# Feed-forward down product of a decoder trunk: two passes of eight output tiles, or seven block products

## The chip, the cores and the metric

The kernel runs on one core of a Trainium2 chip. The metric is device time in microseconds of one execution. Before the change the median of three runs is 2619.1 us (2617.98 to 2620.26).

## The reference, cut to what matters

One decoder layer over 2048 tokens of width 1024: RMSNorm, a token mixer of three head groups (gated linear attention, a recurrent branch, dilated attention), residual; then RMSNorm, a gated feed-forward with a short convolution, residual, and a last RMSNorm. The change touches the last part, and one idle engine inside the dilated attention.

```python
u = rms_norm(x2, norm_ffn) @ w_up            # (2048, 1024) @ (1024, 5632)
u = causal_dwconv(u, conv_w, conv_b)         # width 3
a = gelu(gate) * value                       # (2048, 2816), gate and value are the halves of u
x3 = x2 + a @ w_down                         # (2048, 2816) @ (2816, 1024)
out = rms_norm(x3, norm_final)
```

## The kernel before, in words

All tensors are transposed: channels on the 128 partitions, tokens along the free dimension, in blocks of 512 (NB). A product in float32 is made of three TensorE passes: ScalarE writes a rounded copy ("hi") of each operand, VectorE subtracts it from the raw one ("lo"), and `three_passes` (L2069 to L2071) multiplies hi by hi, hi by lo and lo by hi. Each pass is one matmul of 128x128 weights by 128x512 data.

The program runs four functions in turn: `mixer_front`, `dilated_attention`, `output_projection` and `conv_ffn`. The last takes over half of the time. It works through the tokens in two halves of 1024 (two blocks of 512 each).

**Up stage of a half** (22 pairs g of a value tile and a gate tile): the up product is already done as seven block products per pair (names A00, S1, S2, A01, S3, A11, S4 in `ORDER`), 84 matmuls per pair. GpSimd makes the sums of weights (`sums_of_slab`, `last_sum_of_slab`), ScalarE and VectorE split nine products ahead into a ring of 11 slots (`high_w` L2481, `low_w` L2629). ScalarE keeps partial sums (`keep`, L2491), VectorE moves the four blocks out of PSUM (`move`, L2646 to L2652), ScalarE applies the middle tap (`tap`, L2500), VectorE the two other taps (`convolve`, L2667), ScalarE the GELU (L2505), and VectorE multiplies value by gate (`multiply`, L2674). SyncE stores the product to DRAM (`store_a`, L2247).

**Down stage of a half**: 44 steps (two passes over the 22 tiles of the inner dimension). A pass makes four of the eight output tiles for both token blocks, in all eight PSUM banks. A step loads one weight tile (256 KB) and one activation tile (512 KB) (`load_step`, L2256 and L2258), splits both (`high_step` L2514, L2515; `low_step` L2679, L2681), and runs 24 matmuls (`down`). Raw operands and split operands have two buffers each. After a pass VectorE adds the residual (`drain`, L2689), ScalarE squares (L2524), GpSimd sums the squares (`totals`, L2403); the first four output tiles are written to a scratch tensor x3_t and read again later, since the RMS is known only after the second pass. `sum_squares` (L2811) sums over partitions with a matrix of ones, `root` (L2533, L2535) makes the reciprocal root, `invert` (L2696) and GpSimd (L2427, L2449) scale the output.

Every engine runs its list in the order in which it is written, and waits for semaphores on the way. So the order in the code is the order of the work. The loop over pairs in the vector engine's program ends with the last pair's work in the order: move, `low_step(half, 0)`, move, gate taps, move, `low_step(half, 1)`, value taps, multiply, then the steps from 2 on. SyncE's list has `store_a` of the last pair ahead of the loads of step 2.

**Dilated attention**: 40 turns j; in the first 16 (`TILES_0`) the keys and queries are read in place; GpSimd stages keys only from turn 16 on (`stage`, L1387), and has nothing else to do until then. VectorE works on PSUM (maxima L1531, copies L1537, sums taken L1554, L1556), SyncE stores values and sums of each turn (`store_values` L1310, `store_sums` L1306).

## Time and profile before

| what | value |
|---|---|
| median of 3 runs | 2619.1 us |
| the profiled execution's own time | 2608.52 us |
| its span, first to last instruction | 2606.7 us |
| mean granted TensorE clock | 0.971 |
| dilated attention | from about 683 to 985 us of the span |
| output projection | about 1003 to 1190 us |
| down stage, first half | starts at 1645 us |
| down stage, second half | 2330 to 2581 us |

The profiled execution ran 10.6 us below the median of the runs shown. Matmuls are pipelined: the "busy" time of TensorE says little about its pace, the count of matmuls in a stretch says more. Where a wait is said to end with some engine, that was inferred from the semaphores.

### The profile page before, as it was taken

To read this page: it belongs to the slowest core of one execution; us is meant where nothing else is said; L and a number is where in the kernel's file an instruction comes from. 1 tells how busy PE (TensorE), PEld (TensorE's weight loads), DVE (VectorE), ACT (ScalarE), POOL (GpSimd) and SP (SyncE) were. 2 spreads that over 40 slices of the span, in tenths; PEclk is the share of its full clock that TensorE was granted. 3 is DMA by queue.
4 is the path that set the end of the run, shared out by engine and by line. 5 is a ranking of instruction groups with operands and counts; after the bars stand their busy time and mean duration, and the time that the engine had idled before them with its cause. 6 is when DMAs were issued, how large, how long until landed. Compare 5 with 4: busy or idle time off the path is not lost.

```text
span 2606.7 us, 32959 instructions
## 1 busy us (share of the span) xinstructions
PE 2468.8 (95%) x12224; PEld 1991.9 (76%) x12224; DVE 1557.8 (60%) x2159; ACT 1083.9 (42%) x1859; POOL 736.3 (28%) x648
## 2 busy tenths in 40 slices
PE   7999999999799996995999999899989999999996
PEld 5777777777578775874888888788868888877885
DVE  6554456774355774354777777445567877763434
ACT  6434353332247553124444444225454444432432
POOL 4111104340004761223333332012044534310103
PEclk9999999999899998997999999999999999999998
DMA  4232325442514226354222122465513222224463
GB/s 161 97 109 91 102 88 163 150 148 71 194 57 142 90 78 237 122 186 181 87 82 89 73 96 83 140 210 199 170 73 134 101 89 81 74 87 158 163 242 125
DMA packets 149279, 327.27 MB, mean 126 GB/s; under 512 B 12656, under 2 KB 56704, under 8 KB 141440
## 3 DMA queue, kind: packets, MB, share of 16 engines
q1 hardware_dynamic: 149120, 325.17, 36.3%
q8 instruction: 98, 1.61, 0.3%
q14 instruction: 61, 0.50, 0.1%
HBM read 231.55 MB, written 93.57 MB: 125 GB/s over the span
## 4 chain that ended last, share of the span: by engine, by line
PE 47%; DVE 3%; POOL 1%; ACT 1%; DMA 1%; issue 1%; SPq 0%; POOLq 0%; ACTq 0%; DVEq 0%
PE ff_bank L2069 16%; PE ff_bank L2071 16%; PE ff_bank L2070 16%; DVE ff_y L2667 1%; POOL ffn_rstd L2403 1%; DVE ff_b_lo L2624 1%; POOL ff_x_last L2449 0%; DMA ff_a_raw<-a_t 0%; DMA ff_b_raw<-h_t 0%; ACT ff_y L2500 0%; DVE ff_ring L2629 0%; DVE ff_x2d L2689 0%; DVE ff_a_lo L2681 0%; ACT ff_a_hi L2515 0%; DMA out_t<-ff_x2d 0%
## 5 line engine op out<-in xcount | busy, mean ns | idle before, releaser
L2069 PE MATMUL ff_bank<-ff_b_hi,ff_ring 128*128 128x512 f32 x1232 | 483.9, 393 | 33.5 <-DVE ff_b_lo L2624 13.5
L2071 PE MATMUL ff_bank<-ff_b_hi,ff_ring 128*128 128x512 f32 x1232 | 482.3, 391 | 0.0
L2070 PE MATMUL ff_bank<-ff_b_lo,ff_ring 128*128 128x512 f32 x1232 | 482.2, 391 | 0.0
L66 PE MATMUL ip_bank<-ip_x_hi,ip_w_hi 128*128 128x512 f32 x736 | 302.2, 411 | 19.5 <-DVE ip_x_lo L701 16.1
L2069 PEld LDWEIGHTS ff_bank<-ff_b_hi,ff_ring 128*128 128x128 f32 x1232 | 233.1, 189 | 87.0 <-issue 32.7
L2069 PE MATMUL ff_bank<-ff_a_hi,ff_w_hi 128*128 128x512 f32 x704 | 276.8, 393 | 16.7 <-DVE ff_a_lo L2681 16.5
L67 PE MATMUL ip_bank<-ip_x_lo,ip_w_hi 128*128 128x512 f32 x736 | 292.5, 397 | 0.0
L68 PE MATMUL ip_bank<-ip_x_hi,ip_w_lo 128*128 128x512 f32 x736 | 291.4, 396 | 0.0
L2667 DVE SCALAR_TENSOR_TENSOR ff_y<-ff_u,ff_conv_all,ff_y 128x1024 f32<-128x1024 f32 x176 | 240.3, 1365 | 63.0 <-ACT ff_y L2500 59.8
L2070 PE MATMUL ff_bank<-ff_a_lo,ff_w_hi 128*128 128x512 f32 x704 | 276.0, 392 | 0.0
L2071 PE MATMUL ff_bank<-ff_a_hi,ff_w_lo 128*128 128x512 f32 x704 | 275.8, 392 | 0.0
L2070 PEld LDWEIGHTS ff_bank<-ff_b_lo,ff_ring 128*128 128x128 f32 x1232 | 233.2, 189 | 48.7 <-issue 0.2
L2071 PEld LDWEIGHTS ff_bank<-ff_b_hi,ff_ring 128*128 128x128 f32 x1232 | 233.0, 189 | 48.9
L2629 DVE TENSOR_TENSOR ff_ring<-ff_raw,ff_ring 128x512 fp32r<-128x512 f32 x220 | 177.1, 806 | 61.0 <-ACT ff_ring L2481 61.0
L2679 DVE TENSOR_TENSOR ff_w_lo<-ff_w_raw,ff_w_hi 128x512 fp32r<-128x512 f32 x88 | 63.9, 727 | 245.6 <-ACT ff_w_hi L2514 245.6
L66 PEld LDWEIGHTS ip_bank<-ip_x_hi,ip_w_hi 128*128 128x128 f32 x736 | 141.4, 192 | 56.2 <-issue 15.0
L2514 ACT ACTIVATE ff_w_hi<-ff_w_raw 128x512 fp32r<-128x512 f32 x88 | 55.6, 632 | 304.8 <-PE ff_bank L2071 276.0
L2069 PEld LDWEIGHTS ff_bank<-ff_a_hi,ff_w_hi 128*128 128x128 f32 x704 | 133.5, 190 | 46.8 <-DVE ff_a_lo L2681 18.7
L2500 ACT ACTIVATE ff_y<-ff_u,ff_conv_all 128x1024 f32<-128x1024 f32 x88 | 109.6, 1245 | 135.8 <-DVE ff_u L2650 101.3
L67 PEld LDWEIGHTS ip_bank<-ip_x_lo,ip_w_hi 128*128 128x128 f32 x736 | 141.7, 193 | 30.6 <-issue 2.6
L68 PEld LDWEIGHTS ip_bank<-ip_x_hi,ip_w_lo 128*128 128x128 f32 x736 | 141.5, 192 | 30.7
L1450 ACT ACTIVATE at_probs<-at_s,at_neg 128x256 f32<-128x256 f32 (+1 forms) x288 | 108.1, 437 | 135.6 <-DVE at_neg L1531 121.7
(248 smaller groups left out, 4388.6 us busy)
## 6 DMA issues: line engine op xcount, KB each, us to landing
ff_a_raw<-a_t SPq DMA_DIRECT2D x88, 512.0 KB, 4.2
ff_raw<-in_slabs SPq DMA_DIRECT2D x43, 1024.0 KB, 4.8
proj_t<-ip_staged SPq DMA_DIRECT2D x92, 256.0 KB, 2.7
a_t<-ff_y SPq DMA_DIRECT2D x44, 512.0 KB, 2.6
ff_w_raw<-in_w_down SPq DMA_DIRECT2D x88, 256.0 KB, 2.7
rp_tables<-in_rope SPq DMA_DIRECT2D x24, 512.0 KB, 4.4
ip_w_raw<-in_w_in SPq DMA_DIRECT2D x23, 512.0 KB, 4.0
at_qkv<-proj_t SPq DMA_DIRECT2D x12, 768.0 KB, 12.0
```

Of the source, the lines that this page charges most:

```text
L66: pe.matmul(out, w_hi[k], x_hi[k], start=(k == 0), stop=False)
L67: pe.matmul(out, w_hi[k], x_lo[k], start=False, stop=False)
L68: last = pe.matmul(out, w_lo[k], x_hi[k], start=False, stop=(k == n - 1))
L1450: ins = act.activation(probs[:, g, at], scores_at(j, g)[:, hh, n * c:n * (c + 1)], ACT.Exp, bias=neg[:, j % 2, c, 2 * g + hh:2 * g + hh + 1])
L2069: pe.matmul(out, w_hi, x_hi, start=first, stop=False, skip_group_check=resumed)
L2070: pe.matmul(out, w_hi, x_lo, start=False, stop=False, skip_group_check=resumed)
L2071: return pe.matmul(out, w_lo, x_hi, start=False, stop=last, skip_group_check=resumed)
L2500: act.activation(y[:, a, :], u[:, a, TAPS - 1:], ACT.Identity, bias=conv_all[:, g, a, TAPS:TAPS + 1], scale=conv_all[:, g, a, TAPS - 1:TAP ...
L2514: act.activation(w_hi[n % 2][:, :], w_raw[n % 2][:, :], ACT.Copy).then_inc(d_hi_ready, 1)
L2629: dve.tensor_tensor(ring[:, M % RING, 1, :], source(half, m), ring[:, M % RING, 0, :].bitcast(F32), ALU.subtract).then_inc(w_lo_ready, 1)
L2667: dve.scalar_tensor_tensor(out=y[:, a, :], in0=u[:, a, t:t + HALF], scalar=conv_all[:, g, a, t:t + 1], in1=y[:, a, :], op0=ALU.mult, op1=A ...
L2679: dve.tensor_tensor(w_lo[n % 2][:, :], w_raw[n % 2][:, :], w_hi[n % 2][:, :].bitcast(F32), ALU.subtract).then_inc(d_lo_ready, 1)
```

## The change

- **Down product**: the output of a half is taken as a 2x2 matrix of blocks (four output tiles by 512 tokens), the inner dimension as 11 (`KP`) pairs of tiles. Instead of eight block products it makes seven (`DOWN`), each over 11 steps: 77 steps of 12 matmuls. A step loads one weight tile and one activation tile of 512 tokens, 256 KB each. Raw operands get three buffers, split ones four, in slots of the ring.
- **Sums of weights** (`s_t`, four per pair of tiles): made by GpSimd during the first 16 turns of the attention, in a ring of three, loaded and stored by SyncE between its other transfers.
- **Sums of gated activations** (`t_t`): VectorE makes four per two pairs (`sums_of_gated`), one after an even pair, three after an odd one; ScalarE keeps one block before it is overwritten. SyncE stores them.
- **Partial results**: ScalarE copies the first product out (`keep_first_product`), GpSimd adds it to three quarters of the residual (`add_first_product`), VectorE drains six groups of four tiles.
- **Output**: all eight output tiles of a half stay in SBUF, so the scratch x3_t, its store and its loads go away, and so does GpSimd's scaling (L2427, L2449). The second token block is squared, summed and scaled inside the last steps. For the last block of all, the last four squares are summed over partitions by TensorE directly, one matmul of the ones matrix each.
- **End of the up stage**: step 0's split stands earlier, step 1's too, a third step is split ahead; `store_a` of the last pair and its sums are stored after the loads of step 8.

The core of the diff:

```diff
+W_RING = 3
+            def load_weights(i):
+                if i >= W_RING:
+                    sp.wait_ge(w_stored[i % W_RING], 16 * (i // W_RING))
+                for m in range(2):
+                    sp.dma_start(w_sums[:, i % W_RING, 2 * m:2 * m + 2, :], w_down[m, 2 * i:2 * i + 2].rearrange("k p c -> p k c")
+                                 ).then_inc(w_in[i % W_RING], 16)
+            def store_weights(i):
+                sp.wait_ge(w_summed, 4 * (i + 1))
+                sp.dma_start(s_t[i], w_sums[:, i % W_RING, :, :]).then_inc(w_stored[i % W_RING], 16)
             for j in range(TURNS):
+                if 0 <= j - 5 < KP:
+                    store_weights(j - 5)
+                if 0 <= j - 3 < KP:
+                    load_weights(j - 3)
                 if j < TILES_0:
                     store_values(j)
...
+            def sum_weights(i):
+                pool.wait_ge(neg_saved, i + 3)
+                pool.wait_ge(w_in[i % W_RING], 32 * (i // W_RING + 1))
+                at = w_sums[:, i % W_RING, :, :]
+                pool.tensor_tensor(at[:, 3, :], at[:, 2, :], at[:, 3, :], ALU.add).then_inc(w_summed, 1)
...
+            for i in range(KP):
+                sum_weights(i)
             for j in range(TILES_0 - 1, TURNS + 4):
...
+        DOWN = [("A11", "B11", 0, True), ("A12", "B21", 0, False), ("S2", "T2", 1, True), ("S1", "T1", 0, True),
+                ("S3", "T3", 1, False), ("S4", "B22", 0, False), ("A22", "T4", 1, False)]
+        STEPS = len(DOWN) * KP
...
             def load_step(half, n):
...
+                if n >= 3:
+                    sp.wait_ge(d_lo_ready, 2 * (N - 2))
...
+                for n in range(3, STEPS):
                     load_step(half, n)
+                    if n == 8:
+                        store_a(half, PAIRS - 1)
+                        store_t(half, PAIRS - 1)
+                    if 10 <= n < 26:
+                        load_x(half, n - 10)
+                    if half == 0 and 26 <= n < 42:
+                        load_piece(1, n - 26)
+                    if half == 0 and n in (50, 56):
+                        load_slab(1, (n - 50) // 6)
+                store_out(half, 1)
...
             def tap(half, g, a):
...
+                if G and a == 0 and G % 2:
...
+                    act.activation(t_sum[:, 2, :], y_val[:, blk(1)], ACT.Copy).then_inc(t_kept, 1)
...
             def high_step(half, n):
+                act.wait_ge(d_in[n % 3], 32 * loads_of(half, n))
+                if n >= 4:
+                    act.wait_ge(down_done, OC * (N - 3))
...
+            def sums_of_gated(half, g):
...
+                if g % 2 == 0:
...
+                    dve.tensor_tensor(t_sum[:, 0, :], y_val[:, blk(1)], y_val[:, blk(0)], ALU.subtract).then_inc(t_made, 1)
+                else:
...
+                    dve.tensor_tensor(t_sum[:, 1, :], y_val[:, blk(1)], t_sum[:, 0, :], ALU.subtract).then_inc(t_made, 1)
+                    dve.wait_ge(t_kept, I + 1)
+                    dve.tensor_tensor(t_sum[:, 2, :], y_val[:, blk(1)], t_sum[:, 2, :], ALU.subtract).then_inc(t_made, 1)
...
+                    dve.tensor_tensor(t_sum[:, 0, :], y_val[:, blk(0)], t_sum[:, 1, :], ALU.subtract).then_inc(t_made, 1)
...
                     low_next(2)
+                    if g:
+                        sums_of_gated(half, g - 1)
                     move(half, g, 1)
...
+                low_step(half, 2)
                 convolve(half, PAIRS - 1, 0)
                 multiply(half, PAIRS - 1)
-                for n in range(2, STEPS):
+                sums_of_gated(half, PAIRS - 1)
+                for n in range(3, STEPS):
+                    if n % KP == 3 and 2 <= n // KP <= 6:
+                        drain(half, n // KP - 2)
                     low_step(half, n)
+                    if half == 0 and 33 <= n < 49 and n % 4 == 1:
+                        for i in range(4):
+                            norm_b(n - 33 + i)
+                    if half == 0 and n >= 49:
+                        low_b(1, n - 49)
+                    if n >= 73:
+                        scale_out(half, 1, (2 * (n - 73), 2 * (n - 73) + 1))
...
                 for n in range(STEPS):
+                    if n == 70:
+                        sum_squares(half, 1)
                     down(half, n)
-            sum_squares(1, 0)
-            sum_squares(1, 1)
...
+            pe.matmul(bank, ones[:, :], total[:, blk(0)], start=True, stop=False)
+            for i in range(OC):
+                pe.wait_ge(square_ready, 7 * OC + i + 1)
+                pe.matmul(bank, ones[:, :], squares[:, i % 2, :], start=False, stop=i == OC - 1).then_inc(tail_summed, 1)
```

## Rows read from the trace of the kernel before

**Rows 1.** The page: busy time by engine, and the chain that ended last.
```profile
PE 2468.8 (95%) x12224; PEld 1991.9 (76%) x12224; DVE 1557.8 (60%) x2159; ACT 1083.9 (42%) x1859; POOL 736.3 (28%) x648
...
PE 47%; DVE 3%; POOL 1%; ACT 1%; DMA 1%; issue 1%; SPq 0%; POOLq 0%; ACTq 0%; DVEq 0%
```

**Rows 2.** Windows: PE, PEld, DVE, ACT, POOL busy (instructions), clock, DMA share, GB/s.
```profile
1400.00:1500.00 100.00, 100.00 (x442) 82.81 (x442) 73.89 (x85) 47.05 (x69) 32.79 (x32) 1.00 0.22 80
...
2400.00:2500.00 100.00, 100.00 (x442) 82.81 (x442) 39.55 (x44) 38.87 (x53) 11.77 (x8) 1.00 0.56 190
```

**Rows 3.** Down matmuls, one of three lines: ns min/median/max, first and last start.
```profile
L2069 PE MATMUL ff_bank<-ff_a_hi,ff_w_hi x704: 387/389/796, 1645.0 to 2580.2; 128*128 128x512 f32 x176
```

**Rows 4.** Windows of 5 us after the first half's step 1.
```profile
1655.00:1660.00 5.00, 1.71 (x8) 1.09 (x6) 0.00 (x0) 0.00 (x0) 0.00 (x0) 0.93 0.86 245
1660.00:1665.00 5.00, 0.85 (x2) 0.76 (x3) 2.75 (x4) 3.15 (x4) 0.00 (x0) 0.50 0.98 363
1665.00:1670.00 5.00, 5.00 (x14) 3.85 (x14) 1.00 (x1) 0.00 (x0) 0.00 (x0) 0.55 0.91 322
```

**Rows 5.** Timelines of ScalarE and VectorE, end of the first up stage.
```profile
1648.09 0.61 ACT L2514 ACTIVATE ff_w_hi<-ff_w_raw 128x512 fp32r<-128x512 f32 x1
...
1649.56 1.23 ACT L2500 ACTIVATE ff_y<-ff_u,ff_conv_all 128x1024 f32<-128x1024 f32 x1
...
1650.83 2.60 DVE L2667 SCALAR_TENSOR_TENSOR ff_y<-ff_u,ff_conv_all,ff_y 128x1024 f32<-128x1024 f32 x2
1653.54 1.23 DVE L2674 TENSOR_TENSOR ff_y<-ff_y 128x1024 f32<-128x1024 f32 x1
```

**Rows 6.** Up stage, second half: timelines of VectorE and GpSimd, and a group.
```profile
2230.95 1.18 DVE L2629 TENSOR_TENSOR ff_ring<-ff_raw,ff_ring 128x512 fp32r<-128x512 f32 x1
2234.36 0.69 DVE L2650 COPY ff_u<-ff_bank 128x512 f32<-128x512 f32 x1 [2.23 <-PE ff_bank L2071]
...
2231.65 1.63 POOL L2372 TENSOR_TENSOR ff_s<-ff_s,ff_raw 128x512 f32<-128x512 f32 x1
...
L2650 DVE COPY ff_u<-ff_bank 128x512 f32<-128x512 f32 x11 | 7.6, 692 | 24.5 <-PE ff_bank L2071 24.5
```

**Rows 7.** Down stage: VectorE's weight split, and landings of weight, then activation loads.
```profile
L2679 DVE TENSOR_TENSOR ff_w_lo<-ff_w_raw,ff_w_hi 128x512 fp32r<-128x512 f32 x35 | 24.2, 693 | 109.5 <-ACT ff_w_hi L2514 109.5
...
DMA to landing us min/median/max: 2.5/2.7/6.6
...
DMA to landing us min/median/max: 3.6/4.2/8.1
```

**Rows 8.** Attention: two windows, GpSimd's first wait, a GpSimd sum, VectorE's turns.
```profile
690.00:700.00 10.00, 10.00 (x79) 7.47 (x80) 5.99 (x10) 4.89 (x13) 0.00 (x0) 1.00 1.05 407
...
780.00:790.00 10.00, 10.00 (x82) 7.80 (x81) 5.39 (x9) 4.77 (x12) 0.00 (x0) 1.00 0.11 40
...
803.11 1.61 POOL L1387 COPY at_k_s<-at_qkv 128x384 f32<-128x384 f32 x2 [98.07 <-PE at_s L1652]
...
L2350 POOL TENSOR_TENSOR ff_b_raw<-ff_b_raw 128x512 f32<-128x512 f32 x4 | 5.1, 1282 | 16.6 <-DVE ff_b_raw L2615 16.6
...
L1556 DVE COPY at_o_sb<-at_neg x16: 159/161/422, 697.4 to 805.5; 128x6 f32<-128x6 f32 x16
```

**Rows 9.** Between the halves: windows of 5 us, and ScalarE's table load.
```profile
1905.00:1910.00 5.00, 4.07 (x15) 2.39 (x14) 0.55 (x1) 1.62 (x4) 4.86 (x4) 1.00 0.00 0
...
1915.00:1920.00 5.00, 2.00 (x10) 1.38 (x8) 3.79 (x7) 4.80 (x8) 0.00 (x0) 1.00 0.56 210
...
1909.92 1.28 ACT L2533 ACT_TABLE_LOAD   x1
```

**Rows 10.** Matmuls of ones, the last of them, and landing of 1 MB loads.
```profile
L2811 PE MATMUL ff_bank<-ffn_rstd,ff_ones x8: 590/667/1190, 1905.7 to 2590.2; 128*128 128x512 f32 x8
...
2589.22 2.04 PE L2811 MATMUL ff_bank<-ffn_rstd,ff_ones 128*128 128x512 f32 x2 [4.26 <-POOL ffn_rstd L2403]
...
ff_raw<-in_slabs SPq DMA_DIRECT2D x43, 1024.0 KB, 4.8
```

505 lines of the change are left out of this document (283 added, 222 removed).

## The prediction, written before the changed kernel was run

> **What bounds the kernel now.** I read the page first, for who carries the end: TensorE is busy 95% of the span and its three lines of the feed-forward make 47% of the chain that ended last, with no other engine over 3% [rows 1]. Busy time overstates TensorE, since matmuls overlap, so I went on to windows and counted. In a full stretch of the up stage 442 matmuls fit into 100 us, and just as many in the down stage [rows 2]: one per 0.2262 us in both, with the clock at its full level. Nothing else ends a wait there. So in these stages a matmul less is 0.2262 us less, as long as the engines that feed TensorE keep up with it. Then I looked for where TensorE stops: after step 1 of each down stage, between the halves, and at the end. A difference of 0.2% (5 us) is about what a measurement of this kernel can tell from no change. The sum below stands against the profiled execution (2608.5 us); the median of the runs shown is 10.6 us above it, and I carry that distance over.
>
> **Passes removed.** Before, the down product takes 2 halves x 44 steps x 24 = 2112 matmuls (three lines of 704 [rows 3]). After, 2 x 77 x 12 = 1848. The 264 that go are worth 264 x 0.2262 = **59.7 us**. Shape and type are the same, so this term has one answer.
>
> **Feeding the shorter steps.** A step lasts 12 x 0.2262 = 2.71 us instead of 5.43. VectorE splits two tiles of 512, 0.69 us each [rows 7], 1.4 us; ScalarE does two copies of 0.61 us [rows 5], 1.2 us. Both fit. The first half adds to VectorE a tile of `low_b` in the last 28 steps, four norms in four steps, and 2.7 us of drain in five: with split operands up to three steps (8 us) ahead, and 0.6 to 1.3 us to spare per step, this is caught up. From step 73 on root, low_b and two scales per step come together (some 3.5 us per step against 2.71); I charge **3 us** for it in all (between 0 and 8).
> The loads: 512 KB per 2.71 us are 193 GB/s, and 290 GB/s in the 48 steps that carry a third load (16 of residual in each half, 16 of the next half's input); 363 and 407 GB/s have been granted [rows 4, 8]. A raw buffer's round is issue 0.8, landing about 3.4, two copies and a subtraction 1.9, signals 0.3: 6.4 us against the 8.1 that three buffers give. The landing is between 2.7 (256 KB alone) and 4.2 (512 KB behind 256 KB) [rows 7]. Cost 0.
> The rest of the stage goes together at 0: four copies of the first product by ScalarE (2.4 us once per half, with 8 us of lead), twelve additions by GpSimd at 1.28 [rows 8] spread over 11 steps, the scratch tensor's transfers and GpSimd's scaling gone; all of it lay or lies beside the matmuls. Without the lead the copies would cost their 2.4 us.
>
> **Start of the down stage.** Now step 2 waits: its loads stand behind the store of the last pair, whose multiply ends at 1654.8 [rows 5]. In the 15 us from 1655, 24 matmuls ran instead of 66 [rows 4]: 42 x 0.2262 = 9.5 us, part standing still and part at half clock, and the second half shows the same pattern. After, step 2 is split earlier, and the wait moves to step 3, which VectorE splits only after value taps, multiply and three sums. From these rows: ScalarE splits step 2 from 1648.1 for 1.2, copies a block for 0.6, taps for 1.2 (1651.1); VectorE taps 2.6, multiplies 1.2, makes three sums at 0.6 (1656.9), splits step 3 in 1.3: 1658.2. TensorE wants it at 1645.0 + 3 x 2.71 = 1653.1 [rows 3, 5]. A stand of 5.1 us, and as after the present one the half clock for some 5 us more, 2.7 lost: 7.8 in place of 9.5, so **1.7 us gained per half, 3.4**. The bounds are 19 gained (VectorE in time) and 2 lost.
>
> **Up stage.** VectorE gets four sums per two pairs, ScalarE one copy of 0.6 us that the taps wait for. VectorE's slack is its wait for TensorE ahead of the third move: 24.5 us in 11 pairs, 2.23 us per pair or 4.5 per two [rows 6]. The added work is 4 x 0.6 + 0.6 = 3.0 us bare. But a subtraction of two SBUF operands took 1.18 us instead of 0.68 where GpSimd's sums ran beside it [rows 6], and the new ones stand just where GpSimd still has two of its four to do: with two or three of them stretched by 0.5 it is 4.0 to 4.5 us. That just fits, and nine products of lead cover single lateness. SyncE gets four stores more per two pairs; behind them stand slab loads that wait longer for the split anyway. Cost 0; the bounds are 0 and, with all four stretched and the copy's signals, 6 us against 4.5: 1.5 x 22 = 33 us. I take 0 since the slack row covers the likelier count.
>
> **Attention.** GpSimd idles until 803 us (98 us of it at a stretch) [rows 8]. 44 sums of 1.28 us, four per turn: 5.1 us in a turn of (805.5 - 697.4) / 15 = 7.2 us [rows 8]. The last begins after turn 12's sums are taken, at 697.4 + 12 x 7.2 = 784, and ends at 789; two stagings of 1.6 follow, by 793, and turn 16's scores come near 798. VectorE's work in these turns reads PSUM, so I expect no stretching. SyncE stores a sum one turn after GpSimd has begun it, so its waits for GpSimd hold back no values or sums of the attention. DMA carries 2.1 MB more per turn, 290 GB/s on top of 40; 407 were granted at the stage's start [rows 8]. Cost 0; were the rate only the 190 GB/s of the down stage [rows 2], a turn would last 11 us and 11 turns cost 42 us.
>
> **Between the halves.** Two windows have 15 and 10 matmuls of 22 [rows 9], 4.3 us lost while squares, sums, root with two table loads and scaling of a whole half pass through. After, one block of two is done before the stage ends, but the first kept product waits for that block's store and for two squares. I take half of it, **2 us gained** (0 to 4).
>
> **The end.** Now 2606.7 - 2580.9 = 25.8 us from the last product. After: five sums over partitions of two matmuls of 0.667 us [rows 10], 6.7; root 0.7 and 0.6 with a table load of 1.3 [rows 9] between, 2.6; eight scales of 0.69, 5.5; landing of 1 MB, 4.8 [rows 10]; signals 0.5. Together 20.1, **5.7 us gained** (3 to 8: a second table load, the clock in the last matmuls, which took 2.04 us as a pair [rows 10]).
>
> **Sum.** 59.7 + 3.4 + 2 + 5.7 - 3 = 67.8 us. 2608.5 - 67.8 = 2540.7 for a profiled execution, and 2619.1 - 67.8 = **2551.3 us** as the median.
>
> **Rivals.**
> *VectorE bounds the up stage.* For it: the margin of at most half a microsecond per two pairs [rows 6]. Against: it has lead, and GpSimd's ops may fall elsewhere. 2551.3 + 33 = 2584 us.
> The Trainium skill (GPSIMD Engine Reference, Key points) says that GpSimd shares its SBUF interfaces with VectorE and contends with its instructions that have two SBUF inputs; every added sum is such an instruction, and the 1.18 us row agrees. By that rule the attention, whose VectorE work reads PSUM, stays free.
> *Small loads wait on each other in the 48 steps with a third load.* If three landings of 2.7 us follow one another instead of overlapping, a round takes 0.8 + 8.1 + 2.2 = 11.1 us against 8.1: 1 us per step, 48 us, 2599 us. Against: before, 512 KB behind 256 KB landed in 4.2 us [rows 7].
> The Trainium skill (DMA: Bandwidth & Descriptors, Bandwidth) asks for DMAs of 1 MiB or more for three quarters of the peak, which speaks against 256 KB loads twice as often; this rival is what that rule would do here.
> *Slower than before: every round of raw buffers is late.* Place: the wait of `load_step` for the split of step n - 3. It decides from a landing of 6.4 us on: then a round takes 9.5 us, a step 3.15, and 154 x 0.44 eats the 67.8. At the longest landing seen for an activation load, 8.1 us [rows 7], a step takes 3.7: 154 x 1.0 = 154 us, 2705 us. For it: 290 GB/s is near what was granted. Against: the median is half of that.
> *Attention limited by its DMAs*: 2551.3 + 42 = 2593 us.
> *No stand at the down stage's start*: VectorE finishes in time, 15.6 us better, 2536 us. Against: the order of its list.
>
> **Chances.** Forecast 0.50; no stand 0.12; VectorE-bound up stage 0.20; third load 0.08; attention 0.05; late rounds 0.05. The range runs from the no-stand case to the VectorE-bound one, 2536 to 2584 us, and leaves 0.18 out. All but the late rounds are faster by over 0.2%: 0.94, with 0.01 for a mild form of that case at no change, and 0.05 slower.
>
> **What would show it.** Right: 1848 down matmuls; the up stages still at 442 per 100 us with VectorE's wait ahead of the third move near nothing; down stages at one step per 2.71 us, a stand of about 5 us before step 3; GpSimd's 44 sums over by 790 us and turn 16 at its old time; 20 us after the last product. Wrong: fewer than 440 matmuls per 100 us in the up stage (VectorE bound), ScalarE waiting for loads in the down stage, an attention longer than 302 us.

## The result and the profile after

The changed kernel takes **2602.5 us** as a median (2598.7 to 2604.5, 4 runs) beside 2619.7 for the kernel before in the same series (2618.0 to 2624.6, 4 runs): a ratio of 0.993, 95% interval 0.9912 to 0.9947. It is faster by 17 us; 68 had been forecast, and the range ended at 2584. Its profiled execution took 2602.8 us.

The page of the changed kernel, sections 1 and 4; they answer to [rows 1]:
```profile
PE 2432.7 (94%) x11968; PEld 1950.5 (75%) x11968; DVE 1756.3 (68%) x2411; ACT 1129.6 (43%) x2008; POOL 825.3 (32%) x696
...
DVE 20%; PE 17%; issue 7%; ACT 6%; DMA 1%; POOL 1%; DVEq 0%; SPq 0%; ACTq 0%; POOLq 0%
```
VectorE was 3% of the chain that ended last and is 20% now, while TensorE fell from 47% to 17%: more of the time now hangs on VectorE's work than on any other engine's. Where, the windows of the changed kernel say (a full stretch of the up stage, and one of the second down stage, as [rows 2]):
```profile
1400.00:1500.00 100.00, 97.22 (x428) 79.70 (x427) 86.43 (x91) 45.28 (x68) 36.70 (x30) 1.00 0.29 108
...
2400.00:2500.00 100.00, 98.36 (x435) 81.12 (x434) 65.85 (x86) 46.62 (x82) 24.47 (x16) 1.00 0.74 228
```
428 matmuls in place of 442 in the up stage, at full clock. Starts of the first and last matmuls of the up stages (one row for both halves) and of the down stages (a row for each half), with the kernel before's in [rows 3]:
```profile
L2107 PE MATMUL ff_bank<-ff_b_hi,ff_ring x1232: 387/389/1415, 1222.5 to 2362.5; 128*128 128x512 f32 x176
...
L2107 PE MATMUL ff_bank<-ff_ring x308: 389/389/796, 1674.8 to 1911.6; 128*128 128x512 f32 x154
...
L2107 PE MATMUL ff_bank<-ff_ring x308: 389/389/798, 2363.1 to 2582.0; 128*128 128x512 f32 x154
```
All 1848 down matmuls are there. From such first starts, taken for both kernels, comes this account of the two profiled executions (us). A stage runs to the start of the next. TensorE goes into the second up stage without a pause and stands for the end of the first half only some 6 to 40 us later, so the way between the halves, with its 2 us forecast as gained, is in the up stages' row:

| | before | after | forecast of the difference | measured |
|---|---|---|---|---|
| up to the attention's first matmul | 683.4 | 697.5 | 0 | +14.1 |
| attention and output projection | 523.8 | 525.0 | 0 | +1.2 |
| up stages | 437.8 + 433.5 | 452.3 + 450.9 | -2 | **+31.9** |
| first down stage | 252.0 | 237.5 | | -14.5 |
| second down stage, to its last matmul | 250.3 | 219.3 | | -31.0 |
| both down stages | | | -60.1 | **-45.5** |
| the end | 26.0 | 18.6 | -5.7 | -7.4 |

The first row is code that is the same in both. It took between 683.4 and 698.5 us over the executions profiled in this study, 683.4 and 697.5 in these two: that is why the profiled executions lie only 5.7 us apart (2608.5 and 2602.8) and the medians 17. What has to be explained is the up stages (34 us over the forecast) and the down stages (15 us short of it, all in the first half: the second gained 31.0, about what was asked of it).

The up stages' row holds two things. The first 168 matmuls of the second up stage, with the way between the halves in them, took 50.0 us before and 47.3 after. The rest of that stage went from 383.4 to 403.6 us, and the same part of the first up stage from 381.9 to 396.5, where 1680 matmuls at 0.2262 us make 380.0.

**What costs the up stage.** The sums of gated activations in the changed kernel, all 88 (ns min/median/max, first and last start):
```profile
L2798 DVE TENSOR_TENSOR ff_t_sum<-ff_y_val x22: 679/1781/1786, 1274.3 to 2355.1; 128x512 f32<-128x512 f32 x22
L2803 DVE TENSOR_TENSOR ff_t_sum<-ff_y_val,ff_t_sum x22: 680/1780/1785, 1293.7 to 2373.2; 128x512 f32<-128x512 f32 x22
L2805 DVE TENSOR_TENSOR ff_t_sum<-ff_y_val,ff_t_sum x22: 681/1775/1780, 1295.4 to 2373.8; 128x512 f32<-128x512 f32 x22
L2808 DVE TENSOR_TENSOR ff_t_sum<-ff_y_val,ff_t_sum x22: 680/1774/1777, 1297.1 to 2374.4; 128x512 f32<-128x512 f32 x22
```
The shortest take 0.68 us, the median 1.78. The two timelines of one place, VectorE's and GpSimd's (start, length), show whom they met:
```profile
1451.45 0.68 DVE L2741 TENSOR_TENSOR ff_ring<-ff_s,ff_ring 128x512 fp32r<-128x512 f32 x1
1452.05 0.68 DVE L2741 TENSOR_TENSOR ff_ring<-ff_raw,ff_ring 128x512 fp32r<-128x512 f32 x1
1452.65 1.78 DVE L2803 TENSOR_TENSOR ff_t_sum<-ff_y_val,ff_t_sum 128x512 f32<-128x512 f32 x1
1454.36 1.78 DVE L2805 TENSOR_TENSOR ff_t_sum<-ff_y_val,ff_t_sum 128x512 f32<-128x512 f32 x1
1456.06 1.77 DVE L2808 TENSOR_TENSOR ff_t_sum<-ff_y_val,ff_t_sum 128x512 f32<-128x512 f32 x1
...
1452.28 1.60 POOL L2450 TENSOR_TENSOR ff_s<-ff_raw 128x512 f32<-128x512 f32 x1 [5.37 <-DVE ff_ring L2741]
1453.96 1.63 POOL L2454 TENSOR_TENSOR ff_s<-ff_s,ff_raw 128x512 f32<-128x512 f32 x1
1455.55 1.74 POOL L2455 TENSOR_TENSOR ff_raw<-ff_raw 128x512 f32<-128x512 f32 x1
```
Each VectorE sum stands across one of GpSimd's, and both are longer than alone. GpSimd starts when the split of `low_next(1)` (here at 1451.45) has freed its buffer, and VectorE's sums were put one split later, behind `low_next(2)`: so they meet in every pair for which GpSimd still has sums to make, and of 88, 74 lie beside GpSimd, all 74 of them stretched. And the slack is gone: VectorE's wait for TensorE ahead of the third move, 48.0 us in 21 waits in the first up stage before, is 2.2 us in 3.

**What costs the first down stage.** TensorE's waits in it, changed kernel (total, times, longest):
```profile
PE ff_bank L2107 <- DVE ff_ring L2814: 18.5, 4, 9.9
PE ff_bank L2107 <- ACT ff_e_down L2617: 1.4, 1, 1.4
```
In the second half the same view has 4.9 us in one wait and 1.6. The forecast's stand before step 3 (about 5 us) is there in both halves. The first alone has another of 3.2 us before step 42 and one of 9.9 before step 46; in 1815 to 1825 only 3 matmuls ran, and the granted clock fell to 0.63. ScalarE's timeline there, then GpSimd's:
```profile
1798.20 0.61 ACT L2627 ACTIVATE ff_squares<-ff_x_first 128x512 f32<-128x512 f32 x1
1805.37 1.15 ACT L2610 ACTIVATE ff_ring<-ff_raw_ring 128x512 fp32r<-128x512 f32 x2 [6.56 <-DMA ff_raw_ring<-t_t]
1819.96 0.63 ACT L2627 ACTIVATE ff_squares<-ff_x_first 128x512 f32<-128x512 f32 x1 [13.43 <-POOL ffn_rstd L2493]
...
1808.07 6.36 POOL L2436 TENSOR_TENSOR ff_b_raw<-ff_b_raw 128x512 f32<-128x512 f32 x4 [7.51 <-DVE ff_b_raw L2726]
1814.39 4.92 POOL L2438 TENSOR_TENSOR ff_b_raw<-ff_b_raw 128x512 f32<-128x512 f32 x4
1819.26 0.61 POOL L2493 COPY ffn_rstd<-ff_squares 128x512 f32<-128x512 f32 x1
```
The third square stood 13.4 us in ScalarE's queue, ahead of the roundings of the next steps, since its scratch tile is free only when GpSimd has taken the first square; and GpSimd had its sixteen sums of activations for the second half in front. ScalarE also waits for raw loads, in the whole kernel 67.3 us (38 times) for sums of activations and 55.9 (29) for activations, which made the round of raw buffers a second suspect.

### The profile page after: what moved, and what is told of

The parts are those of the page before. It is cut to its first block, busy times and chain, and to the rows that moved or that the text cites. A ratio compares the mean times of both kernels' runs of the same rounds, so it can differ in the third digit from the quotient of the medians.

```text
span 2601.0 us, 33398 instructions
## 1 busy us (share of the span) xinstructions
PE 2432.7 (94%) x11968; PEld 1950.5 (75%) x11968; DVE 1756.3 (68%) x2411; ACT 1129.6 (43%) x2008; POOL 825.3 (32%) x696
## 4 chain that ended last, share of the span: by engine, by line
DVE 20%; PE 17%; issue 7%; ACT 6%; DMA 1%; POOL 1%; DVEq 0%; SPq 0%; ACTq 0%; POOLq 0%
PE ff_bank L2107 6%; PE ff_bank L2108 6%; PE ff_bank L2109 6%; DVE ff_y_gate L2780 4%; DVE ff_y_val L2780 4%; DVE ff_ring L2741 3%; ACT ff_y_gate L2595 2%; ACT ff_y_val L2595 2%; DVE ff_t_sum L2808 1%; DVE ff_t_sum L2803 1%; DVE ff_t_sum L2798 1%; DVE ff_ring L2814 1%; DVE ff_u L2764 1%; DVE ff_u L2762 1%; ACT ff_ring L2564 1%
## 5 line engine op out<-in xcount | busy, mean ns | idle before, releaser
L2814 DVE TENSOR_TENSOR ff_ring<-ff_raw_ring,ff_ring 128x512 fp32r<-128x512 f32 x308 | 235.8, 813 | 133.5 <-ACT ff_ring L2610 133.5
L2107 PE MATMUL ff_bank<-ff_ring 128*128 128x512 f32 x616 | 244.7, 397 | 26.5 <-DVE ff_ring L2814 23.4
L2610 ACT ACTIVATE ff_ring<-ff_raw_ring 128x512 fp32r<-128x512 f32 x308 | 176.9, 623 | 200.5 <-PE ff_bank L2109 76.9
L2108 PE MATMUL ff_bank<-ff_ring 128*128 128x512 f32 x616 | 242.3, 393 | 0.0
L2109 PE MATMUL ff_bank<-ff_ring 128*128 128x512 f32 x616 | 242.1, 393 | 0.0
L716 DVE TENSOR_TENSOR ip_staged<-ip_bank,ip_rstd 128x512 f32<-128x512 f32 x80 | 54.6, 689 | 175.3 <-PE ip_bank L68 175.0
L2107 PEld LDWEIGHTS ff_bank<-ff_ring 128*128 128x128 f32 x616 | 117.4, 191 | 54.8 <-DVE ff_ring L2814 30.2
L2574 ACT ACTIVATE ff_e<-ff_bank 128x512 f32<-128x512 f32 x132 | 78.2, 592 | 171.7 <-PE ff_bank L2109 169.7
```

The source lines that it names most:

```text
L2107: pe.matmul(out, w_hi, x_hi, start=first, stop=False, skip_group_check=resumed)
L2108: pe.matmul(out, w_hi, x_lo, start=False, stop=False, skip_group_check=resumed)
L2109: return pe.matmul(out, w_lo, x_hi, start=False, stop=last, skip_group_check=resumed)
L2610: act.activation(ring[:, to, 0, :], raw_ring[:, raw_slot(half, n), i, :], ACT.Copy).then_inc(d_hi_ready, 1)
L2814: dve.tensor_tensor(ring[:, to, 1, :], raw_ring[:, raw_slot(half, n), i, :], ring[:, to, 0, :].bitcast(F32), ALU.subtract).then_inc(d_lo_r ...
```

## The experiments

All kernels were measured beside the kernel before (its medians: 2617.8 to 2621.8). Up and down stages in us, from the profiled executions as above; an edit is against the changed kernel unless said.

| kernel | median us | ratio to before, 95% | up | first down | second down |
|---|---|---|---|---|---|
| changed | 2602.5 | 0.993 (0.991 to 0.995) | 452.3, 450.9 | 237.5 | 219.3 |
| e1 sums moved | 2569.1 | 0.981 (0.978 to 0.985) | 437.5, 429.3 | 237.8 | 219.9 |
| e2 squares late | 2596.4 | 0.990 (0.987 to 0.993) | 452.1, 449.6 | 232.2 | 220.1 |
| e4 splits ahead | 2597.7 | 0.992 (0.989 to 0.994) | 452.4, 450.3 | 237.0 | 217.3 |
| e5 sums of 8 columns | 2561.3 | 0.978 (0.975 to 0.981) | 437.5, 429.5 | 234.9 | 217.7 |
| e6 = e1 + e2 + e4 | 2559.9 | 0.977 (0.975 to 0.980) | 437.5, 428.6 | 234.8 | 218.7 |
| e7 = e6, norms spread | 2556.0 | 0.975 (0.972 to 0.978) | 437.7, 429.6 | 226.5 | 221.5 |
| e8 = e7, loads later | 2547.0 | 0.973 (0.970 to 0.975) | 437.6, 427.6 | 226.3 | 215.4 |
| e9 = e6, five buffers | 2546.1 | 0.972 (0.970 to 0.974) | 437.5, 429.2 | 224.9 | 213.0 |
| e10 = e8 + e9 | 2542.1 | 0.970 (0.967 to 0.972) | 438.7, 429.9 | 224.0 | 210.9 |
| e11 five buffers alone | 2603.7 | 0.993 (0.991 to 0.995) | 452.2, 451.7 | 240.2 | 220.0 |
| e12 GpSimd copies | 2560.1 | 0.978 (0.975 to 0.980) | 437.6, 424.7 | 238.7 | 220.9 |
| e13 totals first | 2597.1 | 0.991 (0.990 to 0.993) | 451.9, 451.0 | 232.1 | 220.1 |
| e14 = e2 + e11 | 2599.1 | 0.992 (0.990 to 0.994) | 452.6, 451.0 | 231.5 | 219.6 |
| e15 = e1, e4, five buffers, e13, norms spread | 2547.6 | 0.974 (0.971 to 0.976) | 437.4, 430.1 | 226.4 | 214.6 |

### The up stage: e1, e5, e12

```diff
                     low_next(2)
-                    if g:
-                        sums_of_gated(half, g - 1)
                     move(half, g, 1)
...
                     low_next(5)
+                    if g:
+                        sums_of_gated(half, g - 1)
                     low_next(6)
```


> The changed kernel with one edit: VectorE makes the sums of gated activations one stop later in its list, after the split that follows the gate taps (GpSimd idle there), not after the third split (GpSimd's sums of weights run there). Same work, same count. Theory stretching (each sum takes 1.78 us in place of 0.68 because GpSimd's two-operand sums run beside it): the sums take 0.68 us, two pairs last 38.0 us again instead of 39.7 and 40.4, the up stages shrink from 452 and 451 us to about 438 and 434, the time falls by 25 to 32 us to about 2573. Rival count (VectorE simply has four operations too many per two pairs, wherever they stand): the sums may get shorter but the up stages stay within 3 us of 451, the time within 6 us of 2602.

The sums of e1, and a window of its up stage:
```profile
L2803 DVE TENSOR_TENSOR ff_t_sum<-ff_y_val,ff_t_sum x22: 682/684/691, 1298.3 to 2332.9; 128x512 f32<-128x512 f32 x22
...
1400.00:1500.00 100.00, 100.00 (x443) 82.84 (x442) 80.06 (x98) 46.88 (x70) 34.47 (x31) 1.00 0.31 114
```
The same 88 sums cost TensorE nothing at 0.68 us each, and 36 us in all at 1.78: the up stages are 14.8 and 21.6 us shorter, the median 33 us. Behind their first 168 matmuls both up stages take 381.9 us, no more than before the change. So it isn't the number of sums that binds, it is what they meet.

e5 keeps them in place with 8 of 512 columns each; the rest of each sum is left out. ScalarE's kept copy stays at 512 columns (0.63 us, 22 times), other than the text below says. Two small clearings of the buffer (1.34 us each) come in.

> The changed kernel with the sums of gated activations and the block kept for them cut to 8 columns of 512 (their stores and loads stay, the result of the down product is then not the reference's). All that the sums cost in the up stage is gone, their place in the list stays. If the sums alone are what the up stages lost, these take about 438 and 434 us as before the change and the time is about 2571; if the stores of the sums or the waits around them cost, part of the 32 us stays. Against the moved sums: equal within 5 us by the theory stretching, 25 us or more below them by the rival count.

The up stages are as short as in e1. The medians lie 8 us apart, more than the 5 allowed; 5 of them are in the down stages, where the stand before step 3 falls from 4.9 to 3.3 us because the three short sums stand ahead of that split. Its rows brought a surprise (two of its four sums, and one place in the timelines):
```profile
L2809 DVE TENSOR_TENSOR ff_t_sum<-ff_y_val,ff_t_sum x22: 154/1251/1258, 1291.3 to 2332.3; 128x8 f32<-128x8 f32 x22
L2811 DVE TENSOR_TENSOR ff_t_sum<-ff_y_val,ff_t_sum x22: 152/154/159, 1292.5 to 2332.4; 128x8 f32<-128x8 f32 x22
...
1443.67 1.25 DVE L2809 TENSOR_TENSOR ff_t_sum<-ff_y_val,ff_t_sum 128x8 f32<-128x8 f32 x1
1444.85 0.15 DVE L2811 TENSOR_TENSOR ff_t_sum<-ff_y_val,ff_t_sum 128x8 f32<-128x8 f32 x1
...
1443.30 1.60 POOL L2450 TENSOR_TENSOR ff_s<-ff_raw 128x512 f32<-128x512 f32 x1 [5.37 <-DVE ff_ring L2742]
1444.98 1.31 POOL L2454 TENSOR_TENSOR ff_s<-ff_s,ff_raw 128x512 f32<-128x512 f32 x1
```
A sum of 8 columns, 0.15 us alone, takes 1.25 beside GpSimd: 1.1 more, as the one of 512 columns (1.78 - 0.68). It pays once; the next ones, behind GpSimd's sum, are over in 0.15. So the stretch looks like a wait of about the length of GpSimd's instruction, not like a slower rate. It touches instructions that read two tiles of SBUF. VectorE's moves out of PSUM, with one SBUF input or none, keep their time beside GpSimd's sums of two inputs; in e1, VectorE's move, its next split, and GpSimd's sum beside them:
```profile
1441.61 0.68 DVE L2760 TENSOR_TENSOR ff_u<-ff_bank,ff_e 128x512 f32<-128x512 f32 x1
1442.21 1.18 DVE L2741 TENSOR_TENSOR ff_ring<-ff_raw,ff_ring 128x512 fp32r<-128x512 f32 x1
...
1441.24 1.60 POOL L2450 TENSOR_TENSOR ff_s<-ff_raw 128x512 f32<-128x512 f32 x1 [5.36 <-DVE ff_ring L2741]
```

e12 asks what on GpSimd's side does it. Its four sums per slab become copies (all four lines like this one):
```diff
-                pool.tensor_tensor(s12[:, 1, :], s12[:, 0, :], raw[:, g % 2, 0, :], ALU.subtract).then_inc(s_ready, 1)
+                pool.tensor_copy(s12[:, 1, :], s12[:, 0, :]).then_inc(s_ready, 1)
```


> The changed kernel with GpSimd's four sums of a weight slab in the feed-forward written as copies of one of their inputs, same size, same waits, same outputs (left out: the adding; products of four of seven weights are of other values). It tells whether the stretch of VectorE's sums comes from two SBUF inputs on both engines. Theory 'two inputs against two inputs': VectorE's sums of gated activations fall from 1.78 to 0.68 us where they stand, up stages 437 to 438 and 429 to 430 us, median 2567 to 2573 as in e1. Rival 'any work of GpSimd in SBUF': they stay at 1.2 to 1.8 us, up stages 445 to 452, median 2590 to 2602. The down stages stay at 237 and 219, since the sums of activations there are not touched.

VectorE's sums of e12, and one of GpSimd's copies alone and one beside them:
```profile
L2805 DVE TENSOR_TENSOR ff_t_sum<-ff_y_val,ff_t_sum x22: 684/1095/1097, 1282.5 to 2322.0; 128x512 f32<-128x512 f32 x22
...
1446.20 0.61 POOL L2461 COPY ff_raw<-ff_s 128x512 f32<-128x512 f32 x1
1452.20 0.95 POOL L2450 COPY ff_s<-ff_raw 128x512 f32<-128x512 f32 x1 [5.39 <-DVE ff_ring L2741]
```
Neither theory holds as put. Copies with one input still make VectorE's sums wait, 0.42 us in place of 1.1; and at 1.10 us the up stages are as short as in e1 (381.9 us behind their first 168 matmuls), since 4 x 0.42 and 3.0 of bare work, 4.7 us, is about the slack of 4.5. The 4.6 us by which its second up stage is shorter than e1's come from the way between the halves: TensorE stands 2.8 us there for the total of the squares, for 5.4 in e1. The extra is 0.18 or 0.19 us less than GpSimd's instruction takes alone (1.28 and 0.61): it follows the length of what GpSimd does. What the engines share, and why, no run here shows.

### The first down stage: e2, e4, e11, e13, e14

e2 has the first block's squares at steps 52 to 55, for 44 to 47 (`if 52 <= n < 56: square(half, n - 52)`).

> The changed kernel with one edit: ScalarE's first four squares stand ahead of steps 52 to 55, not 44 to 47. Theory squares (in the first half ScalarE stands 13 us in its square of step 46 because GpSimd sums squares only after its 16 sums of the next half's input, and the split of step 46 stands behind it): the stand of 10 us in TensorE at 1823 us goes, the first down stage shrinks from 237.5 to 220 to 226 us, the time falls by 11 to 17 us to about 2588. Rival loads (the splits wait for their loads, 57 to 67 us of such waits are seen): the down stage stays within 3 us of 237, the time within 4 us of 2602.

5 us of the stage went, of 12 to 17 expected. TensorE's waits for splits fall from 18.5 us in 4 to 14.7 us in 7 (longest 4.9): the one of 9.9 is gone, and small ones came.

e4 puts splits of steps 3 to 5 ahead of the last pair's work:
```diff
                 high_step(half, 2)
+                high_step(half, 3)
                 tap(half, PAIRS - 1, 0)
...
                 low_step(half, 2)
+                low_step(half, 3)
                 convolve(half, PAIRS - 1, 0)
+                low_step(half, 4)
                 multiply(half, PAIRS - 1)
+                low_step(half, 5)
                 sums_of_gated(half, PAIRS - 1)
...
```


> The changed kernel with one edit: at the end of an up stage the splits of steps 3, 4 and 5 stand ahead of value taps, multiply and sums, one before each, instead of behind all of them. Theory order (the stand of 5.0 us before step 3 in each half is VectorE's list, and the half clock behind it costs 2.7 more): the stands fall below 1.5 us, no half clock follows, each down stage is 5 to 8 us shorter, the time falls by 10 to 15 us to about 2590. Rival (loads of steps 3 and 4 are late anyway): the stand stays above 3 us, the time within 4 us of 2602.

The stand at step 3 went: the first 120 matmuls (ten steps) of the two down stages lose 1.1 and 1.5 us over 120 x 0.2262, for 6.8 and 7.3 in the changed kernel. But the rest of the stages lost 5.1 and 3.9 us more, so the stages are only 0.5 and 2.0 us shorter, not 5 to 8. The stand at the copies of the first product (step 11) grew from 1.4 to 3.4 us in the first half; ScalarE came to the split before it after a wait of 2.3 us for its raw load. With e6 the three edits stand together.

> The three edits of e1, e2 and e4 together: sums of gated activations where GpSimd is idle, squares at steps 52 to 55, splits of steps 3 to 5 ahead of the last pair. If the three act on separate places they add: down from the changed kernel's profiled execution by 31.5 (up stages, 437.5 + 429.3), and by 4 to 6 in each of the down stages (e2: first stage 232.2 in place of 237.5; e4: 236.8, but its second stage 2 shorter). Theory 'separate': median 2555 to 2562, first down stage 230 to 233 us. Rival 'the raw buffers' round decides': in the first down stage a stand that is taken away at one step comes back at another, because every late split starts a late load; then the stage stays at 235 to 238 and the median at 2564 to 2569.

The rival took the down stage: 234.8 us, longer than with e2 alone (232.2), and 2559.9 for the median from the up stage's gain. From this I took the round of three raw buffers for the cause, and e7, e8 and e9 go at it: norms one per step; besides that, extra loads four steps later; or five raw buffers.
```diff
-                    if half == 0 and 33 <= n < 49 and n % 4 == 1:
-                        for i in range(4):
-                            norm_b(n - 33 + i)
+                    if half == 0 and 33 <= n < 49:
+                        norm_b(n - 33)
```


> e6, with the sixteen norms of the first down stage one per step (steps 33 to 48) in place of four in every fourth step. Theory 'bursts': four norms at 1.2 to 1.8 us and eight additions of a drain in one step are more than a step's 2.7 us and leave ScalarE without a raw buffer; spread, ScalarE's waits for loads ahead of its copies fall and the first down stage gets 3 to 6 us shorter than e6's. Rival 'sum of the work': VectorE's splits, norms and low_b stretched beside GpSimd's sums of two inputs are too much over the whole stretch, wherever they stand; then within 2 us of e6. If the spread norms keep GpSimd's sixteen sums of activations waiting longer (they wait for the norms), the squares' totals get later and a stand at the last block comes: 2 to 5 us longer.

8.3 us off the first down stage (234.8 to 226.5), more than asked for. The medians of e6 and e7 lie only 4 us apart, with overlapping intervals, so I rest on the stage. How far a down stage can be trusted, the second halves tell: e6 and e7 run the same code from the second up stage on, and their second down stages are 218.7 and 221.5 us. One profiled execution of each was taken, so differences under 3 us in a down stage say nothing by themselves.
```diff
-                    if 10 <= n < 26:
-                        load_x(half, n - 10)
-                    if half == 0 and 26 <= n < 42:
-                        load_piece(1, n - 26)
+                    if 14 <= n < 30:
+                        load_x(half, n - 14)
+                    if half == 0 and 30 <= n < 46:
+                        load_piece(1, n - 30)
...
-                    if n == KP + 3:
+                    if n == KP + 2:
                         keep_first_product(half)
```


> e6, with the residual's loads four steps later (steps 14 to 29), the next half's input four later (30 to 45), norms one per step from 37, squares from 56, and the copies of the first product one step earlier in ScalarE's order. Theory 'third load': the 3 to 4 us stand at step 11 comes from the raw loads landing late while residual loads fill the queues in the catch-up after the start (DMA busy 0.9 to 1.0 there); with four free steps there the catch-up is over before they begin, the stand at step 11 goes in both halves: 3 us per half, median 5 to 7 us under e7's. Rival 'the copies themselves': 2.4 us of ScalarE at once without lead are the stand; one step earlier changes its place, not its size: within 2 us of e7.

The step-11 stand of 3.5 us is gone in both halves. The second stage is 6.1 us shorter than e7's and 3.3 shorter than e6's; the first is as long as e7's, for waits for splits later on grew from 6.8 to 11.1 us. The later loads, the earlier copy, and norms and squares four steps later (not shown) were changed together; which of them it was isn't told apart.
```diff
         def raw_slot(half, n):
-            return slot(half, n % 3)
+            return slot(half, n % 5)
...
-            return slot(half, 3 + 2 * (n % 4))
+            return slot(half, 5 + 2 * (n % 3))
...
-                if n >= 3:
-                    sp.wait_ge(d_lo_ready, 2 * (N - 2))
+                if n >= 5:
+                    sp.wait_ge(d_lo_ready, 2 * (N - 4))
```


> e6, with the ring of eleven tiles cut for the down stage as five raw buffers and three pairs of split tiles in place of three and four. Theory 'round of raw buffers': a load may start two splits earlier, a round may last 13.5 us in place of 8.1, so lateness of VectorE or of a landing no longer comes back as a wait of ScalarE for loads; those waits (67 and 56 us in the changed kernel) fall below 20, and the first down stage, 209 us of matmuls, comes to 218 to 224 us, the second to 215 to 217 up to the last product; median 10 to 15 us under e6's. Rival 'rate': DMA or VectorE is the limit over the stretch with the third load, whatever the buffers; within 3 us of e6. Rival 'lead of split tiles': with two steps of split lead in place of three, the drain of eight and the norms reach TensorE sooner; 3 to 10 us slower than e6.

ScalarE's first wait in the first down stage, changed kernel, then e9:
```profile
ACT ff_ring L2610 <- DMA ff_raw_ring<-t_t: 54.8, 30, 6.6
```
```profile
ACT ff_ring L2610 <- PE ff_bank L2109: 90.8, 61, 5.1
```
With five buffers ScalarE waits for TensorE to free split tiles, as it should, and hardly for loads (3.9 us, twice). The stages are 9.9 and 5.7 us shorter than e6's. That seemed to prove the round of raw buffers; e11 has the five buffers alone.

> The changed kernel with the five raw buffers and three split pairs alone, the sums and all the rest as changed. Theory: the first down stage lost its 28 us over bare matmuls to the round of raw buffers, set off by VectorE's lateness; with five it falls from 237.5 to 225 to 229 us (the stands of 3.4 and 10.1 us at squares stay only where ScalarE itself waits for the totals: the 13.4 us wait at its square is no wait for a load, and may keep 5 to 8 us of it), the second from 219.3 to 214 to 217; up stages stay at 452 and 451; median 2583 to 2590. Rival 'ScalarE's square wait is the main loss': the first down stage stays at 234 to 238 and the median at 2595 to 2600.

My theory fell. e11's first stage, ScalarE's and TensorE's waits:
```profile
ACT ff_ring L2610 <- PE ff_bank L2109: 100.2, 64, 8.2
ACT ff_squares L2627 <- POOL ffn_rstd L2493: 13.4, 1, 13.4
```
```profile
PE ff_bank L2107 <- DVE ff_ring L2814: 19.1, 4, 10.1
```
The waits for loads, 87 us of them in this stage, are gone, and the stage is no shorter. ScalarE's waits for loads had cost nothing here: TensorE still stood for VectorE's work at step 3 and for the square. e13 takes the second away by order alone, with the squares where they were:
```diff
-                if half == 0:
-                    for o in (T1, T2, T4, T3):
-                        combine_b(o)
                 totals(half, range(OC))
                 if half == 0:
+                    for o in (T1, T2, T4, T3):
+                        combine_b(o)
                     sums_of_slab(1, 0)
```


> The changed kernel with one thing moved: in the first half GpSimd adds the four squares of the first finished block before its sixteen sums of activations, not behind them. ScalarE's 13.4 us wait at its square (for GpSimd's total) is what left TensorE without split operands for 10.1 us, with the half clock behind it. Theory 'square behind sixteen sums': that wait falls under 3 us, the 10.1 us stand goes, the first down stage falls from 237.5 by 8 to 14 us, to 223 to 230; the second stage and the up stages stay (451, 219). Median 2588 to 2595. Rival 'the round of raw buffers takes over', as it did when the squares were put later (e2, 5 us gained of 12): 231 to 235 us, median 2596 to 2598. Against both: ScalarE's roundings of the next half's activations then wait for the later sums, from step 50 on: a new wait, 2 to 10 us.

> The changed kernel with e2's later squares and the five raw buffers of e11, nothing else. Each alone gave 5 and 0 us in the first down stage (232.2 and 240.2 against 237.5). Theory 'two causes in series': the squares' wait hides the lateness of raw loads and the reverse, so together they give more than the sum: 222 to 228 us in the first down stage, median 2587 to 2592. Rival 'the splits ahead of the last pair are what gave the ten microseconds in e9': the stage stays at 230 to 235.

e13 gives 232.1 us, by another edit the same as e2's 232.2, and its square waits 4.3 us. Both take away the stand of 9.9 us, the stage gets 5.3 and 5.4 us shorter, and the rest comes back in small stands. And e14 says that these aren't of the raw buffers either: 231.5, so two causes in series are refuted and its rival holds. What e9 has and e14 has not are e4's splits ahead of the last pair (and e1's moved sums). The place fits: of the 15.6 us that five buffers take from e6's two down stages, 12.3 lie in their first 120 matmuls, which lose 8.1 and 4.8 us in e6, 0.3 and 0.3 in e9, but still 6.8 and 6.8 in e14. Five buffers are not the only way to it: with three, e4 loses 1.1 and 1.5 us there. Why e6, with the moved sums beside e4's splits, loses more is open. TensorE's and VectorE's rows of e13:
```profile
PE ff_bank L2107 <- DVE ff_ring L2813: 12.2, 9, 4.9
```
```profile
L2813 DVE TENSOR_TENSOR ff_ring<-ff_raw_ring,ff_ring 128x512 fp32r<-128x512 f32 x63 | 56.7, 945 | 18.2 <-ACT ff_ring L2609 18.0
```
With 63 splits in 1750 to 1850 at 945 ns each (685 alone), VectorE's own work is stretched while GpSimd works on the second half's activations, and TensorE's small stands are for that work. That the stretch is what makes them was not tested by itself.

### Together: e10, e15

> All edits that gained, in one kernel: sums where GpSimd is idle (e1), splits ahead (e4), norms one per step and extra loads later (e7, e8), five raw buffers (e9). If e8's and e9's gains are of separate causes they add: e8 and e9 are each 13 us under e6, so about 2535 us. Theory 'one cause': both gain because a late raw load no longer reaches TensorE, once since it is late less often, once since there is room for it; then the second adds little: 2540 to 2546 us, first down stage 219 to 224 us. What stays in the second half is the end of 18 to 20 us after the last product.

> Sums moved (e1), splits ahead (e4), five raw buffers (e9), GpSimd's totals before its sums of activations (e13), squares where the change had them, norms one per step from step 30. The stands left in e10's first down stage (1.8, 2.2, 1.9, 1.5 us at steps 54 to 62) stand where VectorE's splits and low_b run beside GpSimd's sums of two inputs. Theory 'contention': those sums now run at steps 46 to 56 beside low_b instead of norms, and no drain falls into them, so the stands fall: first down stage 216 to 222, median 2534 to 2540. Rival: ScalarE waits for these sums at its roundings from step 50 on; 224 to 230 us, median 2542 to 2548, no better than e10.

Theory 'one cause' of e10 holds in its numbers: 2542.1 us, first stage 224.0. e10's stages are 0.9 and 2.1 us under e9's, no more than the scatter; that the cause is one is not shown by this. What is left in that stage is seen in a window and a timeline of e10:
```profile
1790.00:1830.00 40.00, 32.52 (x134) 24.29 (x133) 40.00 (x41) 21.87 (x40) 26.99 (x18) 1.00 0.59 171
```
```profile
1797.75 0.74 DVE L2727 SCALAR_TENSOR_TENSOR ff_b_raw<-ff_b_raw,ff_gain,ffn_rstd 128x512 f32<-128x512 f32 x1
1798.41 0.68 DVE L2736 TENSOR_TENSOR ff_b_lo<-ff_b_raw,ff_b_hi 128x512 fp32r<-128x512 f32 x1
1799.02 2.38 DVE L2815 TENSOR_TENSOR ff_ring<-ff_raw_ring,ff_ring 128x512 fp32r<-128x512 f32 x2
1801.32 0.74 DVE L2727 SCALAR_TENSOR_TENSOR ff_b_raw<-ff_b_raw,ff_gain,ffn_rstd 128x512 f32<-128x512 f32 x1
```
VectorE is busy 40 of 40 us, and TensorE gets 134 matmuls where 177 fit. One round of VectorE (norm, low half of an activation, two splits, one of them stretched by a GpSimd sum) takes 3.57 us, against 2.71 for a step. That is the wait that ends last there. e15, with GpSimd's sums over by step 53, has two stands of 2.1 us at steps 50 and 52, where e10 has 2.0 and 1.8 at 54 and 58, and is no better (2547.6). This speaks for too much work in those steps, wherever the sums fall, but it doesn't show it: e15 also lacks e8's later loads and earlier copy. Running GpSimd's sums without meeting VectorE was not tried. e10's second down stage has no such work: 210.9 us, against 208.8 for 923 bare distances of 0.2262.

**e10 beats both kernels**: 2542.1 us, ratio 0.9695 to before (0.9669 to 0.9721). That it lies below the forecast of 2551.3 doesn't make the forecast right: it has other orders and buffers than the kernel that was forecast, and TensorE's stand before step 3, which the forecast had, is gone.

## Why the prediction was wrong

The forecast was 2551.3 us and the range ended at 2584; the kernel took 2602.5. Two terms failed, *Up stage* and *Feeding the shorter steps*.

*Passes removed* held: 1848 down matmuls, at 0.2262 us each where TensorE doesn't stand.

*Up stage* is the term that failed first, at cost 0, and with it over half of the miss (e1 gives back 33 of 51 us): "with two or three of them stretched by 0.5 it is 4.0 to 4.5 us. That just fits". Of 88 sums 74 are stretched, by 1.1: 3.0 + 4 x 1.1 x 74/88 = 6.7 us per two pairs against 4.5 of slack. The up stages are 14.8 and 21.6 us longer than e1's, 1.3 and 2.0 per two pairs (11 in each), so the slack was some 5 us, a little more than the row showed. In the second half 18 of VectorE's splits of weight sums are stretched as well (9.4 us in all, none in the first); that may be why it loses more. Two steps failed in it. The stretch of 0.5 us was read from one split that met only the rest of a GpSimd sum already running (1.18 us); across a whole one it is 1.1. And the count of two or three stretched sums took GpSimd's place for chance, though GpSimd is released by one split of VectorE's list and the sums stand one split further on, so that all four meet one. The rival *VectorE bounds the up stage* named the mechanism and, at 33 us, the size. I gave it 0.20. e1 and e5 confirm it; that its 33 us came so close is partly luck, since both of its terms were too small (6 us of work and 4.5 of slack, for 6.7 and about 5). The whole time lies 18 us above that rival's 2584, as the down stages missed too.

*Feeding the shorter steps* failed next: "with split operands up to three steps (8 us) ahead, and 0.6 to 1.3 us to spare per step, this is caught up". The spare counted splits at 0.69; beside GpSimd's sixteen sums of activations they averaged 0.84 in 1750 to 1850 and the norms 1.13 (e10's round of 3.57 us shows what that makes). After their tenth step the two stages lost 21.7 and 3.2 us over bare matmuls, for 3 charged in both together: the difference is the first half's extra work. And the queue was not followed: the forecast names no wait of ScalarE's four squares for GpSimd, which had sixteen sums in front; it was 13.4 us long and cost TensorE a stand of 9.9 (granted clock 0.63 in 1815 to 1825, 0.86 in the next 10 us), and e13 shows that the order alone is worth 5 us net. What the rest of the 21.7 comes from is only narrowed down: norms one per step gave 8.3 (e7), the stretched splits are seen but were not taken away. *Late rounds of raw buffers* wasn't it: the waits of ScalarE came and cost nothing while others were later (e11). Five buffers counted only behind e4's splits, and there mostly in the first ten steps (e9 against e6, 15.6 us in the two down stages, 12.3 of them there). The landing was put at about 3.4 us; in the first down stage the medians are 3.3 and 3.6 us for weights, 4.8 and 4.4 for activations. *Small loads wait on each other* wasn't it either: the second down stage has sixteen steps with a third load and lost only 3.2 us after its tenth step.

*Start of the down stage* held in its mechanism: a stand of 4.9 us before step 3 in both halves, for 5.1 forecast, set by the list of VectorE's work as written. It gained more than forecast: the first 120 matmuls lost 10.9 and 11.2 us before, 6.8 and 7.3 after, 8.0 us gained for 3.4. *Copies of the first product* at 0 were off by 1.4 and 1.6 us of stand. *Between the halves*: 2.7 us gained for 2 (50.0 to 47.3 us for the first 168 matmuls of the second up stage), though TensorE still stands 5.4 us at 1927 for the total of the squares. Both the loss before (12.0 us, for the 4.3 counted in two windows) and the loss after (9.3) were larger than the forecast took them for, so that the difference came out is partly luck. *The end*: 7.4 gained for 5.7; the sums over partitions took 4.8 us for 6.7 costed (two matmuls on the totals in 1.0 us, eight on the squares directly in 3.8, beside ScalarE's squares). Two table loads of 1.28 stand in it, one more than counted.

*Attention* at 0 held: 775 matmuls in 700 to 800 with the DMA engines busy 0.97 at 332 GB/s, and 319.0 us in place of 319.4 to the output projection. GpSimd's 44 sums ran until 806.7 us, not 790; 14 of that is the later start of the stage, the rest waits for their loads, and turn 16's first scores came 114.3 us after the attention's first matmul, for 114.7 before.

## What to carry to other kernels

When work is added to VectorE beside a GpSimd that reads SBUF, price each instruction that reads two SBUF tiles at its own time plus that of the GpSimd instruction it can meet (less 0.2 us here), and look at what releases both: if it is the same event, or two neighbours in one engine's list, they meet every time. Placing the same sums a few instructions later was worth 33 us here, twice what the change itself brought. A total of waits (ScalarE's 87 us for loads) says nothing of cost until TensorE's own waits are read: take away the longest stand of the bound engine first, and count for each engine what stands in its queue behind a wait for another.

## What the runs showed of the hardware

- VectorE's sums of two SBUF tiles beside GpSimd's: 0.68 us alone, 1.78 beside a sum of two inputs (1.28 alone, 1.60 to 1.74 together), 1.10 beside a copy (0.61 alone, 0.95 together). With 8 columns in place of 512 the addition is the same 1.1 us. It is as if the engines took turns, whole instructions at a time; that is inferred from the lengths.
- VectorE's moves out of PSUM, with one SBUF input or none, are not stretched: in e1, 87 of them lie beside a GpSimd sum of two inputs for over 0.5 us, and none takes more than 0.69 us.
- Copies of one input on GpSimd stretch VectorE too (e12), which I had not expected.
- The same unchanged first part of the program took from 683.4 to 698.5 us between profiled executions. A stage's own length, from start to start, was steadier in the up stages of the kernels that share them (451.9 to 452.6 us in the first, 449.6 to 451.7 in the second), less so in the down stages (218.7 and 221.5 for the same code in e6 and e7).
